# Pair attention with a pair's scores in one block before the value product, and its transposes parted by projection tiles

## The reference

```python
def _dense_causal(q, k, v, scale, cum=None):        # MLA (q, k: 64 + 32 rotary), FOX (cum: log-forget sums)
    s = einsum('bqhd,bkhd->bhqk', q_blk, k) * scale
    if cum_t is not None: s = s + c_q[..., :, None] - cum_t[:, :, None, :]
    s = where(k_pos[None, :] <= q_pos[:, None], s, NEG_INF)
    return einsum('bhqk,bkhd->bqhd', softmax(s, axis=-1), v)
# SWA: the same over the own and the previous 128 keys, minus slope * distance, with a sink in the sum
y = (o * silu(gate)) @ w_out                        # each layer
x = layernorm(ALPHA * x + y)
```

## Time and profile before

| | |
|---|---|
| time, median of 3 runs | 1684.83 us (1684.57 to 1684.91) |
| span of the profiled execution | 1682.5 us |
| PE busy | 1651.9 us, 98% |
| DVE, ACT, POOL busy | 46%, 46%, 39% |
| waits of PE that the profile names | about 24 us in all |

### The profile page before, as it was taken

The page is one execution under the profiler, slowest core; times in us unless marked ns, Lnnn a source line. Parts: engine busy times, 40 slices in busy tenths (PEclk is TensorE's granted clock), DMA queues, the critical chain, the costliest instruction groups (busy, mean ns, idle before and its releaser), DMA issues.

```text
span 1682.5 us, 24607 instructions
## 1 busy us (share of the span) xinstructions
PE 1651.9 (98%) x9349; PEld 1340.9 (80%) x9349; DVE 775.0 (46%) x2038; ACT 767.3 (46%) x1565; POOL 658.7 (39%) x551
## 2 busy tenths in 40 slices
PE   8999999999999999999999999999999999999998
PEld 8777779777888787788777778777788888888877
DVE  3767636566343434336767636888141111001052
ACT  4566724566243535524566635336753222222252
POOL 5333224332243424234332224792154444444423
PEclk9999999999999999999999999999999999999999
DMA  6323144323442322153223145432153333333322
GB/s 171 70 45 77 47 160 134 78 67 68 150 141 76 82 59 79 48 173 110 62 45 85 47 155 154 118 90 74 49 166 101 100 97 92 100 101 88 125 63 88
DMA packets 216048, 161.19 MB, mean 96 GB/s; under 512 B 53755, under 2 KB 197147, under 8 KB 215932
## 3 DMA queue, kind: packets, MB, share of 16 engines
q1 hardware_dynamic: 205904, 130.21, 27.6%
q10 hardware_dynamic: 9804, 29.38, 5.5%
q0 software_dynamic: 224, 0.03, 0.1%
HBM read 148.32 MB, written 11.14 MB: 95 GB/s over the span
## 4 chain that ended last, share of the span: by engine, by line
PE 66%; DVE 8%; ACT 4%; POOL 1%; issue 1%; ACTq 0%; DMA 0%; DVEq 0%; SPq 0%; POOLq 0%
PE banks L530 33%; PE banks L481 6%; PE banks L483 6%; PE banks L482 6%; PE banks L751 3%; PE banks L712 3%; PE banks L766 3%; PE banks L612 3%; ACT AB L1501 1%; DVE misc L2642 1%; ACT G L1630 1%; DVE banks L2344 1%; DVE banks L2333 1%; DVE AB L2346 1%; PE banks L735 1%
## 5 line engine op out<-in xcount | busy, mean ns | idle before, releaser
L2844 POOL TENSOR_TENSOR w_lo<-w_raw,w_hi 128x512 fp32r<-128x512 f32 (+2 forms) x506 | 618.1, 1248 | 995.1 <-ACT w_hi L1371 983.8
L1371 ACT ACTIVATE w_hi<-w_raw 128x1024 fp32r<-128x1024 f32 (+4 forms) x254 | 249.8, 995 | 158.9 <-PE banks L483 101.6
L530 PE MATMUL banks<-XTh,w_hi 128*128 128x512 f32 (+5 forms) x1216 | 279.6, 372 | 4.0 <-DVE XTl L2306 1.4
L530 PE MATMUL banks<-XTl,w_hi 128*128 128x512 f32 (+5 forms) x1216 | 270.9, 365 | 0.0
L530 PE MATMUL banks<-XTh,w_lo 128*128 128x512 f32 (+5 forms) x1216 | 270.7, 365 | 0.0
L530 PEld LDWEIGHTS banks<-XTh,w_hi 128*128 128x128 f32 (+2 forms) x1216 | 207.1, 187 | 48.8 <-issue 6.4
L530 PEld LDWEIGHTS banks<-XTl,w_hi 128*128 128x128 f32 (+2 forms) x1216 | 211.0, 187 | 37.9
L530 PEld LDWEIGHTS banks<-XTh,w_lo 128*128 128x128 f32 (+2 forms) x1216 | 211.0, 187 | 37.3
L481 PE MATMUL banks<-w_hi,OTh 128*128 128x512 f32 (+1 forms) x448 | 173.0, 386 | 0.6 <-DVE QKl L2069 0.5
L483 PE MATMUL banks<-w_hi,OTl 128*128 128x512 f32 (+1 forms) x448 | 167.9, 375 | 0.0
L482 PE MATMUL banks<-w_lo,OTh 128*128 128x512 f32 (+1 forms) x448 | 167.9, 375 | 0.0
(11 more groups left out here) (218 smaller groups left out, 2209.9 us busy)
## 6 DMA issues: line engine op xcount, KB each, us to landing
w_raw<-in_w_gate_up_dram SPq DMA_DIRECT2D x44, 512.0 KB, 3.8
w_raw<-in_fox_w_in_dram SPq DMA_DIRECT2D x30, 512.0 KB, 4.1
w_raw<-in_mla_w_in_dram SPq DMA_DIRECT2D x26, 512.0 KB, 4.9
w_raw<-in_w_in_dram SPq DMA_DIRECT2D x24, 512.0 KB, 3.8
w_raw<-in_w_down_dram SPq DMA_DIRECT2D x22, 512.0 KB, 3.5
w_raw<-in_swa_w_in_dram SPq DMA_DIRECT2D x20, 512.0 KB, 3.8
w_raw<-in_mla_w_out_dram SPq DMA_DIRECT2D x16, 512.0 KB, 3.7
x_spill<-AB ACTq DMA_DIRECT2D x16, 512.0 KB, 2.8
```

The source lines that it names most:

```text
L530: mm = nc.tensor.matmul(o, wt[:, k, :], xt[:, k, lo:hi], start=first and n == 0 and k == 0, stop=last and n == 2 and k == nk - 1, skip_gro ...
L1371: nc.scalar.activation(view(w_hi, u, RING), view(w_raw, u, RAW), ACT.Copy).then_inc(hi_done, 1)
L2844: ins = pool.tensor_tensor(low[at], raw[at], high[at].bitcast(F32), ALU.subtract)
```

## The change

In middle rounds (0 to 6) of the four layers the order is rewritten on three engines. The mixer of the second block keeps the old order (`spread=False`), and so do rounds -2, -1 and 7.

PE now goes: transposes of head 0 (8 in dense layers, 7 in SWA), the first tiles (`fill(i, 1)`), more transposes (dense 2 and 4, SWA 4 and 3), the second tiles (`fill(i, 2)`), the rest of the transposes (dense), then all chunks of scores of pair i+2 in one block, then the value product. DVE takes all the maxima of pair i+2 in one block behind both `norm` calls. ACT copies the transposes out in three groups (two in SWA), with the exponentials between them.

In the dense layers the chunks of scores lie in three pairs of banks (0/1, 2/3, 4/5). The third pair is that of the transposes, so two waits are new: scores chunk 2 waits for ACT to have copied all the transposes, and the first transposes of the next round wait for DVE to have read all the scores.

In MLA both halves of the keys are handled at `fill` position 2 on ACT and DVE (before, the first half at position 5 or 4).

```diff
+                self.apart = not self.window and not sel
+            def s_bank(self, ch, n):
+                return 2 * ch if self.apart else 2 * (n % 2)
...
-                    if c.sch >= 2:
+                    if pr.apart:
+                        if c.sch >= 3:
+                            pe.wait_ge(ps_free, c.sch - 2)
+                        if ch == 2 and c.tch:
+                            pe.wait_ge(pt_free, c.tch)
+                    elif c.sch >= 2:
                         pe.wait_ge(ps_free, c.sch - 1)
...
+                    if pr.apart and x == 0 and ch == 0:
+                        pe.wait_ge(ps_free, c.sch)
...  PE, in the loop over i
+                    if spread and 0 <= i < n_pairs - 1:
+                        step(i, 0)
+                        step(i, 1)
+                        fill(i, 1)
+                        step(i, 3)
+                        step(i, 4)
+                        if pairs[i].window:
+                            step(i, 6)
+                        fill(i, 2)
+                        if not pairs[i].window:
+                            step(i, 6)
+                            step(i, 7)
+                        for ch in range(3):
+                            scores(i + 2, ch)
+                        mix(i)
+                        fill(i, 3)
+                        continue
...  ACT
+                    if spread and 0 <= i < n_pairs - 1:
+                        fill(i, 0)
+                        turned(i, (0, 0), (0, 1))
+                        gated_high(i - 1)
+                        exps(i + 1, 0)
+                        if not c.early:
+                            early()
+                        fill(i, 5)
+                        fill(i, 1)
+                        if pairs[i].window:
+                            turned(i, (1, 0), (1, 1))
+                        else:
+                            turned(i, (0, 2), (1, 0))
+                        exps(i + 1, 1)
+                        fill(i, 2)
+                        if not pairs[i].window:
+                            turned(i, (1, 1), (1, 2))
+                        store(i)
+                        continue
...  DVE
+                    if spread and 0 <= i < n_pairs - 1:
+                        fill(i, 0)
+                        gated_low(i - 1)
+                        fill(i, 4)
+                        norm(i + 1, 0)
+                        fill(i, 1)
+                        fill(i, 2)
+                        if i not in norm_last:
+                            norm(i + 1, 1)
+                        for ch in range(3):
+                            maxima(i + 2, ch)
+                        mixed(i)
+                        if i in norm_last:
+                            norm(i + 1, 1)
+                        fill(i, 6)
+                        continue
```

More of the change, by code:

```diff
@@ L682, in attention, with pair_attention @@
                 c.head += len(heads)
-            def pair_attention(pairs, fill, ahead):
+            def pair_attention(pairs, fill, ahead, spread=True):
                 a0, n_pairs = c.pair, len(pairs)
@@ L711, in scores @@
                                 r = slice(HD * x, HD * x + HD)
-                                mm = nc.tensor.matmul(bank[2 * (c.sch % 2) + x][:, cols], qp[r, pr.q, ts], kp[r, pr.k, ks],
+                                mm = nc.tensor.matmul(bank[b0 + x][:, cols], qp[r, pr.q, ts], kp[r, pr.k, ks],
                                                       start=n == 0 and t == pr.s_chunks[ch][0],
@@ L724, in scores @@
                                 r = slice(HD * x + r0, HD * x + r0 + 4)
-                                mm = nc.tensor.matmul(bank[2 * (c.sch % 2) + x][:, cols], rows[r, 6, ts], rows[r, 7, ks],
+                                mm = nc.tensor.matmul(bank[b0 + x][:, cols], rows[r, 6, ts], rows[r, 7, ks],
                                                       start=False, stop=True, skip_group_check=True)
@@ L728, in scores @@
                             for x in range(2):
-                                mm = nc.tensor.matmul(bank[2 * (c.sch % 2) + x][:, cols], ident_r[:, :], SEL_R[t],
+                                mm = nc.tensor.matmul(bank[b0 + x][:, cols], ident_r[:, :], SEL_R[t],
                                                       start=False, stop=True, skip_group_check=True)
@@ L734, in scores @@
                                     r = slice(HD * x, HD * x + HD)
-                                    mm = nc.tensor.matmul(bank[2 * (c.sch % 2) + x][:, cols], pr.rope[r, ts], kp[r, 7, ks],
+                                    mm = nc.tensor.matmul(bank[b0 + x][:, cols], pr.rope[r, ts], kp[r, 7, ks],
                                                           start=False, stop=n == 1, skip_group_check=True)
@@ L1225, in _ @@
             pe.wait_ge(idx_r, 24)
-            pair_attention(rel_pairs(), fill, mixed_ahead)
+            pair_attention(rel_pairs(), fill, mixed_ahead, spread=False)
             out_rows("out", KD, src, turned=lambda t: HT[t % 2], turn_at=TURNS["rms"], chunk_at=chunk_at, early=early_ff)
@@ L1488, in attention, with pair_attention @@
                 c.head += len(heads)
-            def pair_attention(pairs, fill, exps_first=()):
+            def pair_attention(pairs, fill, exps_first=(), spread=True):
                 a0, n_pairs = c.pair, len(pairs)
@@ L1517, in norm, with turned @@
                     ins.then_inc(pnorm, 1)
-                def turned(i):
+                def turned(i, *only):
                     if i < 0:
@@ L1523, in turned @@
                     for x in range(2):
-                        for js in pr.t_chunks:
+                        for ch, js in enumerate(pr.t_chunks):
+                            if only and (x, ch) not in only:
+                                continue
                             act.wait_ge(pt_done, c.tch + 1)
@@ L1776, in fill @@
                             query(i + 3)
-                            if i > 0:
-                                keys(g, 0)
                         elif pos == 1:
@@ L1782, in fill @@
                                 gate(2)
-                                keys(g, 0)
                         elif pos == 2:
+                            keys(g, 0)
                             keys(g, 1)
@@ L2017, in fill @@
                     advance()
-            pair_attention(rel_pairs(), fill, (2,))
+            pair_attention(rel_pairs(), fill, (2,), spread=False)
             groups_stored(act, c.g)
@@ L2193, in _, with pair_attention @@
             gate_at = {}
-            def pair_attention(pairs, fill, norm_last=(), norm_first=()):
+            def pair_attention(pairs, fill, norm_last=(), norm_first=(), spread=True):
                 a0, n_pairs = c.pair, len(pairs)
@@ L2214, in maxima @@
                         for t in pr.s_chunks[ch]:
-                            o = bank[2 * (c.sch % 2) + x][:, pr.s_col(t):pr.s_col(t) + pr.keys[t]]
+                            o = bank[pr.s_bank(ch, c.sch) + x][:, pr.s_col(t):pr.s_col(t) + pr.keys[t]]
                             ins = nc.vector.tensor_tensor_reduce(pr.score(b, x, t), o, pr.bias(t, x), 1.0, -3e38,
@@ L2512, in fill @@
                         elif pos == 2:
-                            if i < 0:
-                                keys(g, 0)
+                            keys(g, 0)
                             keys(g, 1)
@@ L2725, in fill @@
                     top(48)
-            pair_attention(rel_pairs(), fill)
+            pair_attention(rel_pairs(), fill, spread=False)
             rms_tail(4)
```

1 line of the change is left out of this document (added).

## The result

| | before | changed |
|---|---|---|
| time, median | 1684.7 us (4 runs, 1684.02 to 1684.91) | 1710.15 us (4 runs, 1707.87 to 1712.9) |
| profiled execution | span 1682.5 us | 1707.87 us, span 1706.1, mean granted clock 0.994 |
| MLA rounds 0 to 6, layer 0 | 16.12, 19.43, 16.13, 19.61, 16.13, 14.17, 14.30 | 17.81, 19.76, 17.83, 20.31, 17.83, 15.73, 17.84 |
| MLA rounds 0 to 6, layer 3 | 16.13, 19.53, 16.13, 19.57, 16.13, 14.17, 14.30 | 17.81, 18.60, 17.81, 20.28, 17.83, 15.73, 17.87 |
| SWA rounds 0 to 6 | 17.51, 16.35 four times, 10.91, 12.35 | 15.86, 15.91 four times, 11.32, 16.63 |

The ratio is 1.0151, 95% interval 1.0139 to 1.0163: slower by 25 us. Forecast were 1703.3 and a range up to 1710. A round is counted from its first transposes to the next round's. Rounds 0 to 6 account for the +23.6 us between the two spans: MLA +11.2 and +10.0, SWA +1.3, FOX +1.4, with -0.2 elsewhere.

What follows compares the result with a forecast made beforehand. PE's stream was taken as the bound: busy 98%, clock at full grant. Even MLA +9.5, odd -1.8, MLA rounds 5 and 6 +6.2, FOX +2.2, SWA +2.4 made +18.5 on 1684.83: 1703.3 us, range 1692 to 1710.

Steps and rivals of the forecast that it cites:

- The likeliest case: Whole kernel: the forecast of 1703.3 us, given 0.64, with its own range 1698 to 1708.
- the sum: Four attention layers: 9.5 - 1.8 + 6.2 + 2.2 + 2.4 = +18.5 us, added to the median of 1684.83.
- The step that failed: PE's waits: counted by length alone, as with even MLA rounds going from 16.13 to 17.7; no clock term.
- Even MLA rounds: MLA rounds 0, 2, 4, both layers: next transposes wait for DVE's maxima, 17.7 instead of 16.13, +9.5 in all.
- the nothing I took: PE, scores behind scores: saving taken as nothing, with bounds of nothing and twice 0.18 us a round.
- Odd MLA rounds: MLA rounds 1 and 3: bank wait of 0.42 and 0.18 go, giving 18.9; round 3 loses some 0.4; -1.8 in all.
- MLA rounds 5 and 6: Last middle MLA rounds: waits for ACT's copies, 28.75 against 25.62, +3.1 a layer, +6.2 in all.
- FOX: FOX layer: +0.1 for each of four rounds, round 2 -0.2, rounds 5 and 6 +2.0; +2.2 in all.
- SWA: SWA layer: rounds 0 to 4 0.18 shorter each, -0.9; rounds 5 and 6 23.75 against 20.41, +3.3; +2.4 in all.
- fewer neighbours, no wait: All rounds: PE sets them and wins 0.18 to 0.54 in each of 28; 1670 to 1680, say 1676; chance 0.08.
- only the ends lose: Even rounds' chain ends about when PE arrives, only rounds 5 and 6 lose: +9, 1692 after gains; chance 0.16.
- The lag compounds: DVE's lateness holds ACT next round: 0.5 more in each of 20 rounds, FOX at upper bound, +12, 1715; chance 0.12.

Runs made afterwards that it cites:

- experiments 5: Changed kernel with 20 extra identity transposes behind the value product of MLA rounds 0, 2 and 4 only; 1706.88 us.
- 9: Changed kernel with extra identity transposes: 20 behind the product of MLA rounds 0, 2 and 4, 16 in round 6 of each attention layer; 1701.91 us.
- experiment 3: Changed kernel with rounds 5 and 6 of all four layers back in the old order; 1699.24 us.
- experiment 10: Changed kernel, new order only in MLA rounds 1 and 3 and SWA and FOX rounds 0 to 4, third bank pair only for scores made there; 1679.98 us.
- experiment 1: Changed kernel with the query's low part on DVE moved behind norm of head 1 in even MLA rounds; 1697.28 us.
- experiment 4: Changed kernel with MLA wholly as before (order, banks, place of the keys), SWA and FOX as changed; 1689.85 us.
- experiments 2: Changed kernel with 20 extra identity transposes behind the value product of all even MLA rounds, round 6 included; 1709.44 us.

## Why the prediction was wrong

The direction, the mechanism and the chain of even rounds were right. The likeliest case named 1703.3, and 1710.15 was measured, 6.8 us more and 0.15 over the range. The profiled execution was 5.1 over the sum (spans +23.6 against +18.5).

- **The step that failed** is the one that prices a wait at its own length. Nowhere in the sum or the rivals is there a term for TensorE's clock. The prediction read the row of nines as full grant; a 9 is 90% or more, and that row reads the same in the kernel with six falls. Behind the new waits it falls to 1.2 GHz. By rounds, against the same rounds of experiments 5 and 9: +1.14 (19.76 against 18.62), +1.16 and +1.15 (rounds 3), +1.67 and +1.70 (rounds 6 of MLA). That is 6.8 us in the profiled execution for five falls; the sixth, in SWA round 6, cost nothing ahead of the product (below). With useless matmuls in these waits the same order takes 1701.91, and the profiled span of 1700.0 is +17.5 against before, where the sum said +18.5. Without the five falls the changed kernel's span would be +16.8, so the other terms together were 1.7 too high. That they came so near is in part luck: they missed in both directions, as follows.
- **Even MLA rounds**: predicted 17.7, +1.6 each and +9.5 in all; measured 17.82, +10.1. Each point of the chain came within 0.1 us (query's low part 11.61 against 11.6, maxima to 17.66 against 17.6). PE's own arrival was wrong: 15.58, not 15.95, as scores behind scores save more than the nothing I took. The whole block takes 3.39 (912.81 to 916.20) where 3.72 was used. It changed the wait (2.23 instead of 1.75), not the round.
- **That same saving counts where PE sets the round**: SWA rounds 1 to 4 are 15.91 against 16.35, -0.44 and not -0.18. The bound of nothing to 0.36 on top of 0.18 held it, the value taken was its lower end. Of the 0.44, the scores in one block give 0.19 (1.60 against 0.89 and 0.90 apart), the transposes and their neighbours the rest. With round 0 (-1.65, whose old order was another one, `todo` in the code, which the prediction passed over) SWA's middle won 3.4 where 0.9 was forecast.
- **Odd MLA rounds**: predicted 18.9 and -1.8 in all (the working's own 0.6, and 0.2 in round 3, make -1.6); at full clock 18.62 and 19.15, -2.6; with the falls +0.8.
- **MLA rounds 5 and 6**: predicted 15.6 and in all +6.2; at full clock 15.74 and 16.18, +6.9; with the falls +10.2. PE waits 2.51 ahead of the product, as said, for ACT's copies.
- **FOX**: predicted +2.2, measured +1.4; rounds 5 and 6 to the product's end 39.08 against 39.1. The middle gave -0.7 where +0.2 was taken: in round 3 a wait of 0.65 us for ACT's copies went, which the sum had left out (25.82, now 25.01). Round 6's product was released by DVE's gate (1.98), not by the copies.
- **SWA** rounds 5 and 6 to the product's end: 25.05 against 23.75 forecast. The granted clock was 0.93 in them, but the 1.3 is not the clock's. ACT's high part of the product was placed at 6.4 into round 6 and stands at 7.43, behind DVE's maxima, and the exponentials, the unit and the copies that release PE's product stand behind it in ACT's order. PE had time to spare even at the low clock. On PE the fall begins at the first row, and ACT's row is the second:

```profile
419.69 1.76 PE L764 MATMUL banks<-ident,AB 128*128 128x128 f32 x7 [2.46 <-DVE AB L2294]
...
423.68 0.63 ACT L1583 ACTIVATE OTh<-otmp 128x512 fp32r<-128x512 f32 x1 [5.76 <-DVE otmp L2309]
...
428.31 1.74 PE L779 MATMUL banks<-AB,V 128*64 128x256 f32 x16 [0.80 <-ACT AB L1559]
```

- **Rivals**: "fewer neighbours, no wait" and "only the ends lose" fall with the even rounds' 17.81. "The lag compounds" gave 1715, nearest in number to what was measured, but not by its mechanism: odd rounds above 19.5 were named as its sign and did appear, yet with the clock kept up they are 18.6 and 19.15, so no lag is carried over. The sign was right and the reading of it would have been wrong.
- **The Trainium skill's rule** in "TensorE: Matmul & The Clock Gate", section "Step-by-step: what each phase is for", is that weight loads are pulled ahead of matmuls in flight. Read as the prediction did, that neighbours then cost nothing, it speaks for no gain in SWA's middle. SWA rounds, where PE sets the time in both kernels, became 0.44 shorter with the same matmuls: the trace disagrees with that reading, more strongly than before.

**Open**: whether the fall comes is not fixed by the wait's length. Six even MLA rounds ended in the same 2.23 us wait ahead of an odd round, and three of them were followed by a fall, ahead of layer 0's rounds 1 and 3 and layer 3's round 3. In experiment 3, with the same code up to there, it was layer 0's rounds 3 and 5 and layer 3's round 3. Runs of the changed kernel differ by 5 us (1707.87 to 1712.9) with mean granted clocks of 0.994 and 0.991; that the two longer ones had more falls is likely from this, but they have no trace. What decides it was not tried.

## What to carry to other kernels

On a kernel whose TensorE never rests, a wait of 2 us costs its length and, often (six of ten waits of some 2 us here), a fall of the clock, which took 1.1 to 1.7 us more where the matmuls behind it set the time; a sum of an order change needs that term for each wait, even if the clock row before is full throughout. Bundling scores pays on TensorE only in rounds where VectorE has slack at their end: before moving a block together, look for what then stands ahead of it on the engine that reads it, and change the order only in the rounds that have the room, with buffers given by the same rule. A wait can be filled with useless matmuls to measure what the clock takes, by itself.

## What the runs showed of the hardware

- A wait of 2.23 us on TensorE was followed by a granted clock of 0.51 over the next 3.4 us in one place and by none in another with the same neighbours (layer 3, rounds 3 and 1). In rounds 0 to 6 the shortest wait with a fall behind it was 1.75 us (experiment 10); behind those of experiment 1's even rounds (some 0.7 us) no odd round had one. But behind layer 3 a fall came after waits of 0.98 us at most (experiment 4), so no bound on the wait's length is shown.
- With twenty 128x128 transposes (2.40 us) in that wait, none of the 18 places in experiments 2, 5 and 9 had a fall, where 3 of 6 had one in the changed kernel and 3 of 6 in experiment 3; nobody reads their result.
- At the low clock eight transposes took 1.94 us instead of 1.06, 512-wide matmuls started 0.43 apart instead of 0.23, a value product took 4.07 instead of 2.37.
- Three chunks of MLA scores in one block take 3.39 us, 0.33 less than the same three apart by the lengths of the earlier trace rows.
